# A hybrid encoder layer on one core: RWKV-7's block inverse on 32x32 blocks, and four smaller edits beside it

## The reference, cut to what matters

```
proj = h @ w_in                 # q, k, v, indexer, RWKV's r k v and codes, two gates
att  = dsa_attention(...)       # indexer scores, top-k keys of a query, T5 bias, softmax
rw   = rwkv7_mix(...)           # per head and token:
         sa = S kk ;  S = S * decay - sa b^T + v k^T ;  y = S r
x    = x + (sigmoid(ga) * (att @ w_att_out) + sigmoid(gb) * (rw @ w_rw_out)) @ w_out
x    = x + relu(rms_norm(x) @ w_ff1)^2 @ w_ff2 ;   y = rms_norm(x)
```

## Time and profile before

| | |
|---|---|
| median of 3 runs | 1226.12 us (1221.83 to 1230.08) |
| profiled execution | 1221.72 us, span 1219.9 us |
| mean granted TensorE clock | 0.982 |
| busy: PE, POOL, DVE, ACT | 94%, 49%, 39%, 25% |
| the chain that ended last, by engine | PE 83%, DVE 10%, waiting for nothing shown 3%, POOL 2% |

### The profile page before, as it was taken

The page is one execution under the profiler, slowest core; times in us unless marked ns, Lnnn a source line. Parts: engine busy times, 40 slices in busy tenths (PEclk is TensorE's granted clock), DMA queues, the critical chain, the costliest instruction groups (busy, mean ns, idle before and its releaser), DMA issues.

```text
span 1219.9 us, 25961 instructions
## 1 busy us (share of the span) xinstructions
PE 1152.4 (94%) x10621; PEld 1086.3 (89%) x10629; DVE 481.0 (39%) x838; ACT 305.7 (25%) x585; POOL 593.0 (49%) x773
## 2 busy tenths in 40 slices
PE   4888989989999989999999999999999999999994
PEld 2876889888888889878889999999999999999994
DVE  5235185974254448986234433222100022220113
ACT  4223333443233343333350122222000012110101
POOL 3542265652122215643326655565565565565662
PEclk8999999999699999999999999999999999999998
DMA  5333442221000033122223222222222222222222
GB/s 198 92 75 63 71 96 84 63 72 38 19 21 3 4 101 104 53 69 78 71 91 109 78 77 72 70 77 77 70 78 77 69 78 77 70 77 78 71 69 87
DMA packets 47176, 89.23 MB, mean 73 GB/s; under 512 B 6600, under 2 KB 9040, under 8 KB 46896
## 3 DMA queue, kind: packets, MB, share of 16 engines
q1 hardware_dynamic: 42656, 76.70, 21.0%
q10 hardware_dynamic: 4432, 11.22, 4.2%
HBM read 80.06 MB, written 7.83 MB: 72 GB/s over the span
## 4 chain that ended last, share of the span: by engine, by line
PE 83%; DVE 10%; issue 3%; POOL 2%; ACT 1%; DMA 0%; DVEq 0%; SPq 0%; POOLq 0%; ACTq 0%
PE acc L624 37%; PE acc L625 24%; PE wk L740 3%; PE acc L806 2%; PE acc L804 2%; PE acc L792 1%; PE wk L624 1%; DVE invs L1844 1%; PE wk L625 1%; PE wk L650 1%; PE wk L1090 1%; PE acc L1063 1%; PE wk L1074 1%; PE wk L768 1%; PE acc L757 1%
## 5 line engine op out<-in xcount | busy, mean ns | idle before, releaser
L546 POOL TENSOR_TENSOR w_lo<-w_raw,w_hi 128x512 fp32r<-128x512 f32 x242 | 324.3, 1340 | 20.1
L543 POOL TENSOR_TENSOR w_hi<-w_raw,ones_w 128x32 fp32r<-128x32 f32 x242 | 67.8, 280 | 429.4 <-PE acc L625 409.5
L624 PE MATMUL acc<-h_hi,w_hi 128*128 128x384 f32 x584 | 207.0, 354 | 21.5 <-DVE kxs L1746 9.3
L624 PE MATMUL acc<-h_lo,w_hi 128*128 128x384 f32 x584 | 198.7, 340 | 0.0
L624 PE MATMUL acc<-h_hi,w_lo 128*128 128x384 f32 x584 | 198.7, 340 | 0.0
L625 PE MATMUL acc<-h_hi,w_hi 128*128 128x256 f32 x584 | 164.0, 281 | 0.0
L625 PE MATMUL acc<-h_lo,w_hi 128*128 128x256 f32 x584 | 164.0, 281 | 0.0
L625 PE MATMUL acc<-h_hi,w_lo 128*128 128x256 f32 x584 | 163.8, 281 | 0.0
L544 POOL TENSOR_SCALAR w_hi<-w_raw 128x480 fp32r<-128x480 f32 x242 | 149.1, 616 | 0.0
L624 PEld LDWEIGHTS acc<-h_hi,w_hi 128*128 128x128 f32 x584 | 110.6, 189 | 32.0 <-issue 14.0
L625 PEld LDWEIGHTS acc<-h_hi,w_hi 128*128 128x128 f32 x584 | 110.9, 190 | 0.4
(11 more groups left out here) (383 smaller groups left out, 2229.5 us busy)
## 6 DMA issues: line engine op xcount, KB each, us to landing
w_raw<-w SPq DMA_DIRECT2D x242, 256.0 KB, 2.6
line_scratch<-line ACTq DMA_DIRECT2D x8, 384.0 KB
xT<-xT SPq DMA_DIRECT2D x4, 640.0 KB, 6.0
x<-xT ACTq DMA_DIRECT2D x1, 2560.0 KB, 8.9
y<-x ACTq DMA_DIRECT2D x8, 320.0 KB, 2.6
bias_p<-line_scratch SPq DMA_DIRECT2D x8, 256.0 KB, 4.3
kc<-k_cache SPq DMA_DIRECT2D x8, 256.0 KB, 2.6
vc<-v_cache SPq DMA_DIRECT2D x8, 256.0 KB, 2.7
```

Of the source, the lines that this page charges most:

```text
L543: nc.gpsimd.tensor_tensor(w_hi[:, s, 0:LEAD], w_raw[:, r, 0:LEAD], ones_w[:], ALU.mult).then_inc(w_high, 1)
L546: nc.gpsimd.tensor_tensor(w_lo[:, s, :], w_raw[:, r, :], w_hi[:, s, :].bitcast(F32), ALU.subtract).then_inc(w_split, 1)
L624: mm(out[:, 0:CUT], w_, x_[:, k0 + b, 0:CUT], start=go, stop=end)
```

## The change

1. The inverse is kept in 32x32 blocks, four on the diagonal of the partitions (`block(b)`), until the last level. `pe_part` and `pe_update` issue twice as many matmuls, each 32x32; DVE and ACT handle half as many columns. At level 4 only the off-diagonal block is multiplied, PE copies the diagonal blocks (`pe_diagonal`), and `solve` takes the whole. i = 0 gets one more step for that copy.
2. Units 0 and 2 come first, then 1 and 3; POOL splits all four before h is there (`w_hi_2`, `w_lo_2`), and PE takes tiles 0 and 1 together, group by group (`first_tiles`). All of `h_lo` is DVE's. The sum of squares is four matmul sums. Unit 4's split still waits for three counts of `w_used`.
3. Scores use four banks.
4. Top-k rounds: a tile that `ROUNDS` doesn't name has none now, and had one. 24 instead of 18 lie among the tiles, none in tiles 12 and 16 and from 18 on; one fewer in each of the first 8 steps.
5. In the last norm the sum of squares 6 comes before x's last addition, and DVE makes all eight products.

```diff
-TOPK_IN_STEP = [4] * 7 + [5] + [4] * 4 + [0] * 4
+TOPK_IN_STEP = [3] * 7 + [4] + [4] * 4 + [0] * 4
-ROUNDS = {5: 0, 7: 2, 8: 2, 9: 2, 22: 0, 23: 0, 24: 0}
+ROUNDS = {5: 0, 6: 1, 7: 2, 8: 4, 9: 4, 10: 4, 11: 3, 13: 3, 14: 2, 17: 1}
...
+FIRST_UNITS = (0, 2, 1, 3)
...
             for u in range(SPLIT):
                 split(u, 16, None, u + 1)
-            for k in range(1, KD, 2):
-                pool.wait_ge(h_high, k + 1)
-                nc.gpsimd.tensor_tensor(h_lo[:, k, :], xT[:, k, :], h_hi[:, k, :].bitcast(F32), ALU.subtract).then_inc(h_low[1], 1)
-            split_units(SPLIT, U_GATE + 2)
+            for u in range(2):
+                split(2 + u, 16, None, 3 + u, w_hi_2, w_lo_2)
+            split_units(RAW, U_GATE + 2)
...
-            for src, sem_, count in ((sq_sum, sum_set, KD - 2), (sq[:, 1, :], sq_ready, KD)):
+            for n, (k, sem_, count) in enumerate(((0, sum_set, 1), (2, sum_set, 2), (4, sum_set, 3), (7, sq_ready, KD))):
...
+            def first_tiles(half):
+                his, los = (w_hi, w_hi_2)[half], (w_lo, w_lo_2)[half]
+                pe.wait_ge(w_split, 2 * half + 2)
+                for b in range(4):
+                    k = 4 * half + b
+                    pe.wait_ge(h_low[k % 2], k // 2 + 1)
+                    for t in range(2):
+                        w_h, w_l = his[:, t, b * P:(b + 1) * P], los[:, t, b * P:(b + 1) * P]
+                        for n, (w_, x_) in enumerate(((w_h, h_hi), (w_h, h_lo), (w_l, h_hi))):
...
+                        if b == 3:
+                            done.then_inc(w_used, 1)
...
-                    if u >= 2 and u % 2 == 0:
-                        pe.wait_ge(sc_relu, u)
+                        pe.wait_ge(line_ready, 1)
+                    if u >= 4 and u % 2 == 0:
+                        pe.wait_ge(sc_relu, u - 2)
-                    mm(wk[:, h % 2, 0:P * (q + 1)], qit[r, h // 2, q * P:(q + 1) * P], kit[r, 0:P * (q + 1)],
+                    mm(wk[:, u % 4, 0:P * (q + 1)], qit[r, h // 2, q * P:(q + 1) * P], kit[r, 0:P * (q + 1)],
...
             def pe_part(i, level, p):
                 for j in range(4):
-                    for c in range(2):
-                        done = mm(acc[half(c), p, j * HD:(j + 1) * HD], merge[n % 2][half(c), 4 * p + j, :],
-                                  invs[i % 2][half(c), p, 0, j, :], start=True, stop=True)
+                    for b in (range(4) if level < 4 else (0, 2)):
+                        to, cols = (b, b % 2) if level < 4 else (b + 1, 1)
+                        done = mm(acc[block(to), p, j * HB:(j + 1) * HB], merge[n % 2][block(b), 4 * p + j, block(cols)],
+                                  invs[i % 2][block(b), p, 0, j, :], start=True, stop=True)
...
             def pe_update(i, level, p):
+                if level == 4:
+                    for j in range(4):
+                        for b in (1, 3):
+                            at_ = 512 + j * HD + HB
+                            done = mm(acc[block(b - 1), p, at_:at_ + HB], part[block(b), 4 * p + j, :], inv_t[block(b), j, :],
+                                      start=True, stop=True)
+                else:
+                    for j in range(4):
+                        for b in range(4):
+                            if i or level < 2:
+                                mm(acc[block(b), p, 512 + j * HB:512 + (j + 1) * HB], inv_t[block(b), j, :],
+                                   part[block(b), 4 * p + j, :], start=True, stop=True)
+                            done = mm(acc[block(b), p, 640 + j * HB:640 + (j + 1) * HB], part[block(b), 4 * p + j, :],
+                                      inv_t[block(b), j, :], start=True, stop=True)
...
+            def pe_diagonal(i, p):
+                pe.wait_ge(inv_set, 2 * added(i, 3 if i else 2) + p + 1)
+                for b in range(4):
+                    out = acc[block(b), p, 512:768].rearrange("q (j d) -> q j d", j=4)[:, :, block(b % 2)]
+                    done = mm(out, ident[block(b), block(b)], invs[i % 2][block(b), p, 1, :, :], start=True, stop=True)
...
                     for c in range(KD):
+                        if c >= 2:
+                            add_squares(c - 1, 2)
                         dve.wait_ge(w_used, u0 + (c + 1) * n_units)
                         V.tensor_tensor(x1[:, c, :], x1[:, c, :], tile_acc[c % 2], ALU.add).then_inc(acc_read, 1)
-                        if c >= 2:
-                            add_squares(c - 1, 2)
...
-            for k in range(0, KD, 2):
+            for k in range(KD):
                 x = x1[:, k, :]
                 dve.wait_ge(y_weighted, k + 1)
                 do(V.tensor_tensor(x, x, rstd2[:], ALU.mult), y_out)
```

More of the change, by code:

```diff
@@ L116, in stream_at, with sums @@
     return u
+FIRST_UNITS = (0, 2, 1, 3)
+def sums(norm):
+    return 3 + (KD - 2) * norm
 def bucket(rel):
@@ L192, in stage, with added, inverted @@
     return (5 * i - 2 if i else 0) + level
+def added(i, level):
+    return stage(i, level) + (1 if i else 0)
+def inverted(i):
+    return 2 * added(i, 5 if i else 4)
 def g_sets(i):
@@ L742, in _, with block @@
             QUADRANTS = ((0, 0), (1, 1), (0, 1), (1, 0))
+            def block(b):
+                return slice(HB * b, HB * b + HB)
             def pe_pairs(i, which):
@@ L794, in pe_part @@
                 done.then_inc(part_mm, 1)
             def pe_update(i, level, p):
-                n, last = stage(i, level), level == merges(i) - 1
-                pe.wait_ge(part_set, 2 * n + p + 1)
+                pe.wait_ge(part_set, 2 * stage(i, level) + p + 1)
                 inv, inv_t = invs[i % 2][:, p, 0], invs[i % 2][:, p, 1]
-                for j in range(4):
-                    for c in range(2):
-                        if not last:
-                            mm(acc[half(c), p, 512 + j * HD:512 + (j + 1) * HD], inv_t[half(c), j, :], part[half(c), 4 * p + j, :],
-                               start=True, stop=True)
-                        done = mm(acc[half(c), p, 768 + j * HD:768 + (j + 1) * HD], part[half(c), 4 * p + j, :],
-                                  inv_t[half(c), j, :], start=True, stop=True)
@@ L934, in _ @@
                     pe_update(0, level, p)
+            for p in range(2):
+                pe_diagonal(0, p)
             pe_from_v(0)
@@ L1168, in x1_stat @@
             def x1_stat(norm):
-                for src, sem_, count in ((x_sum, sum_set, (KD - 2) * (norm + 1)), (x_sq, sq_ready, KD * (norm + 1))):
+                for src, sem_, count in ((x_sum, sum_set, sums(norm)), (x_sq, sq_ready, KD * (norm + 1))):
                     pe.wait_ge(sem_, count)
@@ L1393, in act_first @@
                     act.wait_ge(first_turned, 2 * i + p + 1)
-                    do(A(columns(invs[i % 2][:, p, 0]), acc[:, p, 512:768], ACT.Copy), inv_first)
+                    do(A(invs[i % 2][:, p].rearrange("q n j d -> q (n j d)"), acc[:, p, 512:768], ACT.Copy), inv_first)
             def act_part(i, level):
@@ L1398, in act_part @@
                     act.wait_ge(part_mm, 2 * stage(i, level) + p + 1)
-                    do(A(columns(part[:, 4 * p:4 * p + 4, :]), acc[:, p, 0:256], ACT.Copy), part_set)
+                    do(A(columns(part[:, 4 * p:4 * p + 4, :]), acc[:, p, 0:4 * HB], ACT.Copy), part_set)
             def act_g(i, rows):
@@ L1837, in dve_inverse @@
             def dve_inverse(i, level, p):
-                dve.wait_ge(update_mm, 2 * stage(i, level) + p + 1)
-                if level == merges(i) - 1:
-                    dst, src = invs[i % 2][:, p, 1].rearrange("q j d -> q (j d)"), acc[:, p, 768:1024]
+                dve.wait_ge(update_mm, 2 * added(i, level) + p + 1)
+                if level == (4 if i else 3):
+                    mask = e_masks[:, E_LT + P * (i == 0) + HD:E_LT + P * (i == 0) + P]
+                    do(V.tensor_tensor(solve[i % 2][:, p], acc[:, p, 512:768].rearrange("q (j d) -> q j d", j=4), over_heads(mask, 4),
+                                       ALU.mult), inv_set)
+                    return
+                if level == 2 and not i:
+                    dst, src = invs[i % 2][:, p, 1].rearrange("q j d -> q (j d)"), acc[:, p, 640:768]
                 else:
-                    dst, src = invs[i % 2][:, p].rearrange("q n j d -> q (n j d)"), acc[:, p, 512:1024]
+                    dst, src = invs[i % 2][:, p].rearrange("q n j d -> q (n j d)"), acc[:, p, 512:768]
                 do(V.tensor_tensor(dst, dst, src, ALU.add), inv_set)
```

121 lines of the change are left out of this document (62 added, 59 removed).

## The result

The changed kernel takes 1242.67 us (median of 4 runs, 1241.30 to 1249.56) against 1223.97 us for the kernel before on the same chip: ratio 1.0152, interval 1.0094 to 1.0210. It is slower; 1213 us had been forecast. The profiled execution, the slowest of its runs, has a span of 1246.9 us against 1219.9 us, 27.0 us more, at a mean granted clock of 0.946 against 0.982.

The account below looks back on a forecast made before the run. PE, busy 94% of the span, was taken to bound the kernel; start -6.5, scores -5.7, top-k rounds -0.3, end -1.7 and inverse +1 sum to -13.2 us: 1213 us as median, 8 times in 10 between 1198 and 1264 us.

Parts of the forecast that it names:

- the price of a 32x32 record: RWKV stage's inverse on PE: 16 ns for each of 4320 records, 69 against 64 us, +5 us; bounds 14.5 and 29 ns.
- the inverse's term: RWKV stage: 32x32 blocks, dearer records against shorter copies and waits, +1 us in all, bounds -6 and +61.
- Rival 1: RWKV stage: small tiles drop the clock to half for 40 to 70% of it, +21 to +45 us, 1246 us; chance 0.25.
- Rival 2: Inverse: a record keeps its cost whatever its size; 29 ns gives 1269 us, 21 ns gives 1235 us; chance 0.15.
- Rival 3: Inverse: records in four row groups run side by side at 8 ns, 1179 us, believed as far as 1196; chance 0.08.
- Start: Up to tile 2: four sums of squares and two tiles together, tile 2 at 40.5 us; -6.5 us, bounds -8 and -5.
- Scores: Score matmuls on PE: with four banks the six waits for ACT's reads go; -5.7 us, bounds -5.7 and -3.
- Top-k rounds: DVE's rounds ahead of the three kxs waits: first wait 2.4 us longer, others shorter; -0.3 us, bounds -4 and +3.
- End: Last norm: a sum of squares leaves the chain, 0.8 us, eight products on DVE, 0.9; -1.7 us, bounds -2 and -0.8.
- Its waits and copies: Inverse: DVE's addition falls from 686 to 421 ns, ACT's copy by about 0.1 us, 4.6 us of waits go.
- what would show it: Signs: tile 2 near 40.5 us, longest kxs wait over 6 us, 64 pe_update records in about 1 us, row tile about 30.

Follow-up runs that it names:

- e4: Kernel before plus six streams of unused fp32 matmuls behind its last PE matmul; 32x32 with 32 columns over four row groups: 128 records in 3.47 us.
- e7: Changed kernel with two of four 32x32 blocks in pe_part and pe_update up to level 3, inverse incomplete: 1207.41 us, ratio 0.9854.
- e3: Changed kernel plus 36 unused 128x128 matmuls with 384 columns before the waits of pe_part from level 1: 1239.07 us, ratio 1.0145.
- e10: Kernel before with the start's edits alone (first two tiles together, early POOL splits, four sums of squares): 1212.62 us, ratio 0.9945.
- e2: Changed kernel with the 64x64 inverse put back, so the other four edits alone: 1204.15 us, ratio 0.9871 against the kernel before.
- e11: e6 with POOL's splits of units 4 and 5 waiting for two counts of w_used instead of three and four: ratio 0.9811 against before.
- e14: e11 with PE's five small transposes of the indexer's weights behind tile 2 instead of before it: ratio 0.9838 against before.
- e6: e5 with tile 11's three top-k rounds and mask moved behind tile 14: ratio 0.9770 against before.
- e13: e4 with other streams, such as 32x32 and 64x64 alternating: 160 ns a record one by one, 27 ns in runs of eight.
- e8: e2 with one unused 32x32 matmul ahead of each 64x64 matmul of pe_part and pe_update, 1024 more: 1805.20 us, ratio 1.48.
- e5: e2 with POOL's third and fourth split waiting until ACT has made the first h_hi: ratio 0.9863 against before.

## Why the prediction was wrong, by its own steps

**The failed step is the price of a 32x32 record in the inverse's term.** I took 16 ns for all 4320 of them and +1 us; the stage lost 34.9 us. Worked out my way (64 us before, 34.9 more, 2.5 of waits gone) the mean price was some 23.5 ns a record. What I left out of the sum is the supply of instructions. The 29 ns of the earlier trace rows are the 64x64 matmul's own pace over two row groups (e4, without a gap), and I looked for the lower bound of the new ones in a burst of nine. A burst shows what PE can do with records that it has; it can't show how fast new ones come. The record itself is far cheaper than I took (8.5 ns at full clock), and 128 of them are not to be had in under 3.3 to 3.5 us. Where levels follow each other with nothing between, that is 27 ns a record, my upper bound nearly; where large matmuls lie between, PE catches up. Of the 34.9 us, 24.2 are more time without work and 10.7 more busy time.

**Rival 1, the clock, happened as an event and not at its price.** The clock is at half for some 96 us of the stage instead of 20, as far as the rival said, and its 1246 us is near the result. But e7 has nearly the same clock (0.80) and a stage 36 us shorter, e3 has 0.92 and is 1.6 us shorter in the stage with 23 us of extra work, and the period of a packet is the same at either clock. It stays open how much of the 10.7 us of busy time is the clock's. The Trainium skill, "TensorE: Matmul & The Clock Gate", Part 1, says the gate follows how busy the array has been; e4 agrees in part: one row group of 32x32 ran at 0.50, four with 256 columns at 1.00. **Rival 2** had the mean price between its two values (29 and 21 ns) for a wrong reason: no 32x32 record has a floor of 25 or 29 ns. The Trainium skill, "TensorE: Matmul & The Clock Gate", section "Wait — 56ns, not 53.3ns?", would have about 25 ns from start to start; the runs show 8.5 ns within a packet and 27 ns over many. **Rival 3** believed in 8 ns a record; PE did deliver that within a packet, and it bought nothing, for the want of the next.

**Start**: -6.5 us forecast, -6.7 us measured (e10), in size right, in its parts not. The four sums gained the 3.1 us that I gave as the far bound: ACT's root begins at 15.49 us, not 18.59. Then POOL's splits, "hidden by DVE's root", took it back: in the kernel after the third step of the root takes 1.77 us instead of 0.83 and two scalings 3.11 instead of 1.68.

```profile
17.24 1.23 DVE L1722 SCALAR_TENSOR_TENSOR nrm<-nrm,rstd 128x640 f32<-128x640 f32 x1
17.89 1.71 POOL L567 TENSOR_TENSOR w_lo<-w_raw,w_hi 128x512 fp32r<-128x512 f32 x1
18.51 1.77 DVE L1724 SCALAR_TENSOR_TENSOR rstd<-nrm,rstd 128x640 f32<-128x640 f32 x1
...
20.31 3.11 DVE L1740 SCALAR_TENSOR_TENSOR xT<-xT,vec,rstd 128x640 f32<-128x640 f32 x2
```

Tile 0's first matmul comes at 24.30 us, where I had 23.2. Tile 2 starts at 42.98 us here and at 40.4 to 40.6 in e2, e7 and e10, forecast 40.5; against e2 the first matmul comes 1.4 us later and the clock stays at half for 2.2 us more of the two tiles. The gap before tile 2 is 1.8 us, forecast 1.2, and not unit 4's split alone, as I had it; e11 and e14 show ACT's copies behind it.

**Scores**: 5.5 of the 5.7 us of waits are gone, as forecast, and no later wait took their place. **Top-k rounds**: the first kxs wait grew to 4.6 us from 4.0, not to 6.4; the second grew to 2.5 us, which I had shrinking; the third fell by 1.6 us, forecast 1.8; the sum went from 9.3 to 9.6 us against a forecast of -0.3. What I left out is that such a wait is paid again as clock, so the shape of the waits mattered more than their sum. e6 is the measure: with the three rounds of tile 11 moved behind tile 14 the first wait is 1.6 us instead of 4.6 and the time 10.9 us less. The same omission shows in the profile of the changed kernel: start, scores and rounds should have brought the RWKV stage forward by 12.5 us and brought it forward by 6.5, with 27.2 us at half clock ahead of it instead of 13.6 (6.8 us of work). In e2, with 10.2 us at half, it came 16.5 us sooner. **End**: -1.7 us forecast, -2.1 us in every trace with this edit (16.5 us behind the last MLP matmul against 18.6). The eight products take 5.97 us, as computed to 0.3 us.

```profile
1236.91 5.97 DVE L2147 TENSOR_TENSOR x<-x,rstd 128x640 f32<-128x640 f32 x8
```

Without the inverse my terms add up to -14.2 us; e2 measured -15.7. **Its waits and copies**: DVE's addition takes 420 ns as forecast (421), and 2.5 of the 4.6 us of waits went. The addition came out as forecast, the waits by half, and neither mattered.

Of the list "what would show it", tile 2 near 40.5 us, the scores and the end came out in most traces; the first kxs wait did not. 64 records of one `pe_part` took 0.75 us (0.56 from the first start to the last) and 64 of one `pe_update` 0.7 to 0.9 us from start to start, no worse than the 1 us that I named, but the row tile took 41 us at a clock of 0.79, which I had put down as the sign of rival 1. So the sign that was to vindicate the price came, and the time did not: it lay between the groups.

## What to carry to other kernels

Before halving the size of matmuls, count PE's records per microsecond, not the time of one: where the stretch already runs near 128 records in 3.5 us, more and smaller ones are slower however cheap each is, and gaps marked "issue" one packet of instructions apart are the sign. A wait of 2 us and more ahead of large matmuls can cost half its length again and more, because the clock falls behind it; look at the windows after each wait before rating two waits as equal. When two tiles are run together, ask what their separate ends used to cover. The lowest ratio has e6, the four other edits with later splits and tile 11's rounds moved: 1197.55 us, 2.3% under the kernel before.

## What the runs showed of the hardware that I had not expected

- Instructions reach PE in packets of 16 KB, 128 records, one in 3.3 to 3.75 us when it uses them up faster (e4 and the kernel after), at either clock; it starts on one 1.2 to 1.6 us after the load has landed.
- 32x32 matmuls with 32 columns over four row groups run at 8.5 ns a record at full clock within a packet; 64x64 over two at 29.2 ns, with 32 columns as with 64; 32x32 in one row group at 53 ns at half clock (33.1 us for 623).
- A change of tile size between neighbouring matmuls costs some 0.25 us at half clock (an estimate from e13); alternating ones made a stage of 173 us one of 769 (e8).
- The RWKV stage of the 64x64 kernels, the same code in all of them, comes in two lengths, by whether the clock falls for 17 us behind the sample matmuls as in the earlier trace rows: 172.7 to 174.8 us with the fall (the kernel before, e2, e6, e10, e14), 166.7 us in e5 without, and in e11:

```profile
251.10:417.50 166.40, 156.74 (x4073) 143.49 (x4074) 72.82 (x136) 52.16 (x111) 35.53 (x28) 1.00 0.10 30
```
